# Where block 1 normalises x, and which engines split the expert biases

## The reference

```python
y = xf * lax.rsqrt(jnp.mean(xf * xf, axis=-1, keepdims=True) + RMS_EPS)
return (y * g.astype(jnp.float32)).astype(x.dtype)        # rmsnorm
gu = xblk @ w_gate_up[e] + b_gate_up[e]                    # per expert, 32 experts, 4 per token
gate = jnp.minimum(gu[:, :D_EXPERT], SWIGLU_LIMIT)
up = jnp.clip(gu[:, D_EXPERT:], -SWIGLU_LIMIT, SWIGLU_LIMIT)
act = gate * jax.nn.sigmoid(SWIGLU_ALPHA * gate) * (up + 1)
return act @ w_down[e] + b_down[e]
```

## Time and profile before

| | us |
|---|---|
| median of 3 runs (lowest, highest) | 1533.14 (1532.16, 1533.45) |
| the profiled execution | 1532.21 |
| its span | 1530.3 |
| TensorE busy (matmul), share of the span | 1444.2, 94% |
| VectorE busy | 325.5, 21% |
| ScalarE busy | 216.8, 14% |
| GpSimd busy | 21.5, 1% |
| mean granted TensorE clock | 0.981 |

### The profile page before, as it was taken

The page is one execution under the profiler, slowest core; times in us unless marked ns, Lnnn a source line. Parts: engine busy times, 40 slices in busy tenths (PEclk is TensorE's granted clock), DMA queues, the critical chain, the costliest instruction groups (busy, mean ns, idle before and its releaser), DMA issues.

```text
span 1530.3 us, 17933 instructions
## 1 busy us (share of the span) xinstructions
PE 1444.2 (94%) x7236; PEld 780.0 (51%) x7236; DVE 325.5 (21%) x864; ACT 216.8 (14%) x398; POOL 21.5 (1%) x14
## 2 busy tenths in 40 slices
PE   7999999999999999999999999999699996999998
PEld 5655444444344343334334334334498854888843
DVE  5535311111121111111112112111313344000001
ACT  1321011111111011111101101111213331100000
POOL 3200000000000000000000000000000000000000
PEclk9998999999999999999999999999799996999999
DMA  9997899999999999999999999999943221444400
GB/s 325 354 416 292 340 425 430 427 430 427 429 428 429 428 429 428 427 430 427 430 428 429 427 429 427 430 429 428 316 143 127 84 84 55 138 146 157 137 0 27
DMA packets 82569, 496.95 MB, mean 325 GB/s; under 512 B 6237, under 2 KB 47914, under 8 KB 54666
## 3 DMA queue, kind: packets, MB, share of 16 engines
q1 hardware_dynamic: 81932, 495.46, 79.7%
q10 hardware_dynamic: 606, 1.06, 0.2%
HBM read 495.44 MB, written 1.05 MB: 324 GB/s over the span
## 4 chain that ended last, share of the span: by engine, by line
PE 60%; DMA 34%; DVE 4%; ACT 1%; issue 1%; SPq 0%; DVEq 0%; ACTq 0%
DMA ring<-in_w_gate_up_dram 33%; PE PS L821 16%; PE PS L1137 10%; PE PS L930 6%; PE PS L847 5%; PE PS L1144 5%; PE PS L807 3%; PE PS L713 2%; PE PS L855 2%; PE PS L1012 2%; PE PS L665 2%; PE PS L543 1%; PE PS L560 1%; DVE pt L1566 1%; DMA ring<-in_w_ada_dram 1%
## 5 line engine op out<-in xcount | busy, mean ns | idle before, releaser
L821 PE MATMUL PS<-ring,work 128*64 128x512 f32 x2048 | 451.7, 596 | 13.7 <-DMA ring<-in_w_gate_up_dram 13.6
L821 PEld LDWEIGHTS PS<-ring,work 128*64 128x64 f32 x2048 | 145.2, 137 | 302.5 <-issue 259.9
L847 PE MATMUL PS<-ring,work 128*64 128x512 f32 x1024 | 225.1, 592 | 0.0
L1823 DVE TENSOR_SCALAR work<-PS 128x512 f32<-128x512 f32 x32 | 22.1, 692 | 660.7 <-PE PS L821 660.7
L1137 PE MATMUL PS<-cols,ring 128*128 128x256 f32 x704 | 155.4, 384 | 2.1 <-issue 2.1
L1137 PEld LDWEIGHTS PS<-cols,ring 128*128 128x128 f32 x704 | 135.8, 193 | 22.0 <-DVE cols L1527 2.5
L847 PEld LDWEIGHTS PS<-ring,work 128*64 128x64 f32 x1024 | 72.0, 137 | 131.7 <-issue 129.3
L807 PE MATMUL PS<-work,rows 128*128 128x64 f32 x1056 | 124.9, 278 | 0.0
L807 PEld LDWEIGHTS PS<-work,rows 128*128 128x128 f32 x1056 | 123.8, 196 | 0.8 <-DVE work L1801 0.8
L930 PE MATMUL PS<-ring,cols 128*128 128x240 f32 (+1 forms) x448 | 95.0, 370 | 2.1 <-DVE cols L1527 2.1
L930 PEld LDWEIGHTS PS<-ring,cols 128*128 128x128 f32 x448 | 84.9, 193 | 8.1 <-DVE cols L1527 2.5
(11 more groups left out here) (284 smaller groups left out, 919.3 us busy)
## 6 DMA issues: line engine op xcount, KB each, us to landing
ring<-in_w_gate_up_dram SPq DMA_DIRECT2D x128, 2048.0 KB, 22.1
ring<-in_w_down_dram SPq DMA_DIRECT2D x64, 2048.0 KB, 19.5
ring<-in_w_ada_dram SPq DMA_DIRECT2D x24, 1024.0 KB, 17.2
ring<-in_w_gate_up_dram SPq DMA_DIRECT2D x22, 1024.0 KB, 5.0
ring<-in_w_in_dram SPq DMA_DIRECT2D x13, 960.0 KB, 10.8
ring<-in_w_down_dram SPq DMA_DIRECT2D x11, 1024.0 KB, 4.8
ring<-in_w_out_dram SPq DMA_DIRECT2D x8, 1024.0 KB, 10.2
ring<-in_w_in_dram SPq DMA_DIRECT2D x3, 1024.0 KB, 14.4
```

Source lines behind the costliest of these rows:

```text
L821: mm = pe.matmul(bank(b)[CAP * h:CAP * (h + 1), :], xg[:, k, :], w[:, b * FE + h * 512:b * FE + (h + 1) * 512], start=False, stop=(k == KD ...
L847: mm = pe.matmul(bank(3)[CAP * h:CAP * (h + 1), :], lhs, w[:, (f % 2) * D + h * 512:(f % 2) * D + (h + 1) * 512], start=False, stop=(f == 7))
```

## The change

It has two parts.

*Block 1 turns x as it lands.* `turn_x` transposes x itself, once the constants and x0 or x1 have landed; the constants are now loaded first. VectorE takes the mean square of row tile 0 and ScalarE that of row tile 1. The column copies multiply by the gain as before. The root is computed afterwards for both tiles at once (`attn_r`), and ScalarE applies it when it copies the projected chunks out, one instruction per row tile instead of one for both. `ADA_FIRST, ADA_NEXT, ADA_MID` are 0, 2, 16: no ada chunk stands ahead of `w_in`, and eight instead of six come after the output projection.

*The expert biases.* `b_gate_up` is loaded behind the last of the 34 chunks, after the scores of the eighth head; the copies to bfloat16 are on ScalarE, ahead of the FFN norm's column copies, and the subtractions on VectorE, ahead of the residual add. GpSimd's program is gone.

Besides, three small loads signal `gfin_in` instead of a semaphore of their own, and the counts waited for are adapted (`rows_ready`, `x_squared`).

```diff
-ADA_FIRST, ADA_NEXT, ADA_MID = 2, 4, 18
+ADA_FIRST, ADA_NEXT, ADA_MID = 0, 2, 16
 # SyncE
+            load_small(cst[:, 0:CONST_FIRST], consts[:, 0:CONST_FIRST], "const_in")
             load_small(x_sb[:, 0, :], x_rows[:, 0, :], "x0_in")
             load_small(x_sb[:, 1, :], x_rows[:, 1, :], "x1_in")
-            load_small(cst[:, 0:CONST_FIRST], consts[:, 0:CONST_FIRST], "const_in")
...
-                if n == 3:
-                    for i in range(3):
-                        load_small(bgu_f[32 * i:32 * i + 32, :], ins["b_gate_up"][0], "bgu_in")
...
+            sp.wait_ge(sig["scores_done"], HEADS)
+            for i in range(3):
+                load_small(bgu_f[32 * i:32 * i + 32, :], ins["b_gate_up"][0], "bgu_in")
 # TensorE
+            def turn_x():
+                for t in range(NT):
+                    pe.wait_ge(sig[("x0_in", "x1_in")[t]], 16)
+                    for k in range(KD):
+                        mm = pe.transpose(bank(k // 2)[:, (k % 2) * T + t * P:][:, 0:P],
+                                          x_sb[:, t, k * P:(k + 1) * P], ident)
+                        if t == NT - 1 and k % 2:
+                            mm.then_inc(sig["rows_turned"], 1)
+                turned[0] += 1
...
             pe.wait_ge(sig["const_in"], 16)
+            turn_x()
...
-            for i in range(ADA_FIRST):
-                ada(i)
-            turn_rows(2)
...
             ada(ADA_MID + 3)
+            ada(ADA_MID + 4)
             pe.wait_ge(sig["x_added"], 4)
-            turn_rows(4)
-            ada(ADA_MID + 4)
+            turn_rows(2)
+            ada(ADA_MID + 5)
...
             mm.then_inc(sig["parts_done"], 1)
-            ada(ADA_MID + 5)
+            ada(ADA_MID + 6)
+            ada(ADA_MID + 7)
...
-            pe.wait_ge(sig["bias_split"], 2)
+            pe.wait_ge(sig["bias_split"], 6)
 # ScalarE
+            act.wait_ge(sig["x1_in"], 16)
+            do.tell(nc.scalar.activation(rows[:, 1, :], x_sb[:, 1, :], ACT.Square,
+                                         accum_out=stat(ms, S_ATTN)[:, 1:2]), "x_squared")
             act.wait_ge(sig["vec_cols"], 1)
+            keep_cols(lambda k: col("g_attn_norm", k))
...
-            keep_proj(proj1, IN1_CHUNKS, (4, 5), N_IN1)
+            act.wait_ge(sig["attn_r"], 1)
+            for c, (a, w) in enumerate(IN1_CHUNKS):
+                act.wait_ge(chunk_used, N_IN1 + c + 1)
+                for t in range(NT):
+                    ins_ = nc.scalar.activation(proj1[:, t, a:a + w], bank(4 + c % 2)[:, t * w:(t + 1) * w], ACT.Copy,
+                                                scale=stat(rs, S_ATTN)[:, t:t + 1])
...
-            act.wait_ge(sig["bias_split"], 1)
             for b in range(4):
...
+            act.wait_ge(sig["bgu_in"], 48)
+            act.wait_ge(sig["bdown_in"], 48)
+            for i, hi in enumerate((96, 64, 32)):
+                if i:
+                    act.wait_ge(sig["bias_left"], 2 * i - 1)
+                do.tell(nc.scalar.copy(bias_b[0:hi, :], bgu_f[0:hi, :]), "bias_split")
+                if i:
+                    act.wait_ge(sig["bias_left"], 2 * i)
+                do.tell(nc.scalar.copy(bdown_b[0:hi, :], bdown_f[0:hi, :]), "bias_split")
             keep_cols(lambda k: vcol[:, GFFN_AT + k:GFFN_AT + k + 1])
 # VectorE
-            norm_rows(S_ATTN, 0)
+            do.step(v.tensor_tensor_reduce(out=rows[:, 0, :], in0=x_sb[:, 0, :], in1=x_sb[:, 0, :], scale=1.0,
+                                           scalar=0.0, op0=ALU.mult, op1=ALU.add,
+                                           accum_out=stat(ms, S_ATTN)[:, 0:1]))
...
-            norm_rows(S_ATTN, 1)
             keep_cols(lambda k: col("g_attn_norm", k))
+            dve.wait_ge(sig["x_squared"], 1)
+            at = slice(0, NT)
+            src, dst = stat(ms, S_ATTN)[:, at], stat(rs, S_ATTN)[:, at]
+            do.step(v.tensor_scalar(src, src, 1.0 / D, EPS, ALU.mult, ALU.add))
+            rsqrt(dst, src, rsqrt_tmp[:, at])
+            do.tell(v.tensor_copy(dst, dst), "attn_r")
...
                 do.tell(v.tensor_scalar(att[:, t, :], att[:, t, :], ratio[:, t:t + 1], None, ALU.mult), "att_rows")
+            for i, hi in enumerate((64, 32)):
+                for j, (parts, full) in enumerate(((bias_b, bgu_f), (bdown_b, bdown_f))):
+                    dve.wait_ge(sig["bias_split"], 2 * i + j + 1)
+                    do.tell(v.tensor_tensor(full[0:hi, :], full[0:hi, :], parts[0:hi, :], ALU.subtract), "bias_left")
 # GpSimd: its whole block (copies and subtractions) is taken out
```

More of the change, by code:

```diff
@@ L159 @@
 out_half x_added scores_done rowmax_ready probs_ready smat_ready probs_turned pt_kept pv_done o_free att_rows att_turned att_cols
-pool_steps up_steps o_up_steps o_steps parts_done parts_kept logits_done shifted exp_ready routed ranks_done
+bias_left up_steps o_up_steps o_steps parts_done parts_kept logits_done shifted exp_ready routed ranks_done
 lists_ready bias_split
-picked sel_ready selb_ready seld_ready gathered xg_ready clipped sig_ready act_ready act_turned actt_ready yb_ready
+attn_r picked sel_ready selb_ready seld_ready gathered xg_ready clipped sig_ready act_ready act_turned actt_ready yb_ready
 sel_turned selt_ready scattered
@@ L166 @@
 moe_done x_summed x_squared z_ready r_ready x_scaled ff_ready ff_ln decay_ready cum_done cum_kept cumt_turned bias_rows conv_in conv_turned
[L167 removed]
+conv_sum conv_tanh conv_silu qk_sq heads_ready heads_turned heads_cols ml_exp ml_m ml_guard ml_tanh
 bcast_done bcast_kept y_turned y_kept gate_used silu_ready h_ready out_ready out_stored""".split()
@@ L705, in adas @@
                 return [lambda i=i: ada(i) for i in range(lo, hi)]
-            attention_1({0: adas(6, 8), 1: adas(8, 9), 2: [pool_sums] + adas(9, 10), 3: adas(10, 12), 4: adas(12, 14),
-                        5: adas(14, 16), 6: adas(16, 17), 7: adas(17, ADA_MID)})
+            attention_1({0: adas(4, 6), 1: adas(6, 7), 2: [pool_sums] + adas(7, 8), 3: adas(8, 10), 4: adas(10, 12),
+                         5: adas(12, 14), 6: adas(14, 15), 7: adas(15, ADA_MID)})
             def out_columns(base_n, c, k, t, halves=(0, 1)):
@@ L914, in _ @@
                 add_zero(4 + 2 * t, 5 + 2 * t, start=False, stop=True).then_inc(sig["moe_done"], 1)
-            turn_rows(6)
+            turn_rows(4)
             need_cols()
@@ L1084, in _ @@
             out2(1, 2)
-            pe.wait_ge(sig["rows_ready"], 7)
+            pe.wait_ge(sig["rows_ready"], 5)
             pe.wait_ge(sig["pt_kept"], heads[11][0] + 1)
@@ L1121, in _ @@
             out2(1, 7, (1,))
-            turn_rows(9)
+            turn_rows(7)
             need_cols()
@@ L1209, in _ @@
             do.tell(nc.scalar.activation(trig[:, :, :, :], trig[:, :, :, :], ACT.Sin), "trig_ready")
-            keep_proj(proj1, IN1_CHUNKS, (4, 5), N_IN1)
+            act.wait_ge(sig["attn_r"], 1)
[4 more added lines that the diff above has]
+                                                scale=stat(rs, S_ATTN)[:, t:t + 1])
+                    if t:
+                        do.tell(ins_, "proj_kept")
+                    else:
+                        do.step(ins_)
             flat_q = q_rows.rearrange("p t h n -> p t (h n)")
@@ L1708, in attention_1 @@
                           lambda t: bank(4 + t).rearrange("p (h d) -> p h d", h=HEADS))
-            attention_1({0: [lambda: keep_ada(0), square_pooled], 1: [keep_pooled], 3: [keep_pool_sums],
-                         5: [lambda: keep_ada(1)]})
+            attention_1({0: [square_pooled], 1: [keep_pooled], 2: [lambda: keep_ada(0)], 3: [keep_pool_sums],
+                         7: [lambda: keep_ada(1)]})
             st = stat(ms, S_MIX)
@@ L1890, in _ @@
                         do.step(ins_)
-            dve.wait_ge(sig["gfin_in"], 16)
+            dve.wait_ge(sig["gfin_in"], 64)
             for t in range(NT):
                 do.tell(v.tensor_tensor(z_rows[t], x_sb[:, t, :], gfin[:, :], ALU.mult), "z_ready")
-            dve.wait_ge(sig["x_squared"], 2)
+            dve.wait_ge(sig["x_squared"], 3)
             r_ = rstd(S_FINAL, D)
-            dve.wait_ge(sig["x_squared"], 4)
+            dve.wait_ge(sig["x_squared"], 5)
             st = stat(ms, S_NORM1)
@@ L1927, in _ @@
             dve.wait_ge(sig["proj_kept"], len(IN1_CHUNKS) + R_GATES)
-            dve.wait_ge(sig["bias14_in"], 48)
+            dve.wait_ge(sig["gfin_in"], 64)
             def bias_of(a, n):
@@ L2064, in _ @@
                 add_gated(0, t, "out_ready", 2, N_END)
-        @block.gpsimd
-        def _(pool):
-            steps = 0
-            for parts, full, loaded in ((bias_b, bgu_f, "bgu_in"), (bdown_b, bdown_f, "bdown_in")):
-                pool.wait_ge(sig[loaded], 48)
-                for hi in (96, 64, 32):
-                    done = sig["pool_steps"] if hi > 32 else sig["bias_split"]
-                    nc.gpsimd.tensor_copy(parts[0:hi, :], full[0:hi, :]).then_inc(done, 1)
-                    if hi > 32:
-                        steps += 1
```

(5 more changed lines are left out.)

11 lines of the change are left out of this document (4 added, 7 removed).

## The result

The changed kernel takes 1537.71 us (median of 7 runs, 1533.85 to 1542.74) against 1532.16 us of the kernel before in runs alternating with it (7 runs, 1529.23 to 1533.45): ratio 1.0041, with a 95% interval of 1.0025 to 1.0058. It is slower, by about 6 us. The forecast was 1539.0.

A forecast was written before the change was run, and what follows sets the result against it. The weight stream bounds the kernel from expert 0's first slot release. Second row tile +4.1, ada chunk +0.9 and clock +1.0 give +6.0 us on 1532.21, 1538.2; on the median 1539, own range 1535 to 1543, with rivals 1531 to 1545.

The forecast's parts named there:

- What bounds the kernel: Expert loop: the weight stream limits from 157.86 us, expert 0's first slot release; moving that moves the end equally.
- The start: Block 1 up to attention: TensorE about 6 us earlier (bounds 4 and 7.5), in-projection starting at about 11.4 us.
- The landing of the biases: Late gate/up bias load behind the last ada chunk (108.9): costs 5.2 us of stream, lands at 114.1 (110.8 to 117).
- The split: Bias copies on ScalarE and subtractions on VectorE after the landing: 9.7 us, VectorE free at 123.8 us.
- TensorE's wait for the second row tile: FFN norm: second row tile ready at 135.6 instead of 131.08, transposes done at 136.6, 4.1 us later than before.
- the clock's term: TensorE's clock from the last transposes through expert 0: +1.0 us, between 5.9 us less and 4 us more.
- Ada chunks and clock: Behind the output projection: one moved ada chunk on the path, +0.93 us; TensorE's clock, +1.0 us.
- clock returns: Rival, chance 0.13: biases late as forecast, but two ada chunks restore full clock for expert 0; +2.6 us, 1536.
- The sum: Whole kernel: second row tile +4.1, ada chunk +0.9, clock +1.0, together +6.0 us; 1538.2, forecast on the median 1539.
- Biases out of the way: Rival, chance 0.20: biases land by 105 us or VectorE's share is hidden; TensorE's path decides, 4 us faster, 1529.
- Worse of both: Rival, chance 0.11: biases land at 117 and everything up to expert 0 runs at 1.2 GHz; +12 us, 1545.
- a GpSimd that was slow but in nobody's way: Bias split before the change: GpSimd's work held nobody up; two engines replace it, one in the way.

The follow-up runs named there:

- e7: e3 with the ada chunks placed as before (six behind the output projection, not eight): 1527.56 us, ratio 0.9972.
- e1: The changed kernel with the gate/up bias loaded early and split on GpSimd, as before the change: 1532.37 us, ratio 1.0005.
- e2: The kernel before with only the bias part of the change; start and ada chunks as before: 1536.24 us, ratio 1.0048.
- e5: The changed kernel run again, nothing altered: 1538.32 us, ratio 1.0050 to the kernel before.
- e3: The changed kernel with the three gate/up bias loads issued on ScalarE's DMA queue instead of SyncE's: 1527.96 us, ratio 0.9982.
- e6: e2 with the three gate/up bias loads on ScalarE's queue: 1531.12 us, ratio 0.9997.
- e4: The changed kernel, late load on SyncE's queue kept, bias copies and subtractions on GpSimd again: 1541.79 us, ratio 1.0075.
- e9: The changed kernel, late load on SyncE kept, without VectorE's four subtractions and ScalarE's waits for them (output wrong): 1528.71 us, ratio 0.9983.

## Why the prediction was right, step by step

**What bounds the kernel.** Right. In the two profiles of the changed kernel and the ten of the variants, the time from the first release to the last expert's issue is 868.8 to 870.4 us, 869.48 before, and the span moves with the first release to within what the rest of the kernel varies: from the last of these issues to the end it is 499.9 us (e7) to 503.0 (before). So two profiles whose first releases lie less than 3 us apart can't be ranked by them. The expert at the end still takes 29.37 us.

**The start.** Forecast about 6 us earlier up to attention (4 to 7.5), worth nothing. Measured 4.9 to 5.0 in the first profile and 4.3 to 4.4 in the second: x is turned slower than priced (3.65 us for the 16 transposes instead of 1.97), and the in-projection takes 1.7 and 3.0 us longer, where I took 1 for the low clock. The step that rests on GpSimd's silence is borne out by e1, and more strongly than I priced it: 3.40 us of waiting, not 1.17. "Worth nothing" holds in e2 against e5. With the biases out of the way it seems to be worth something, by e3 against e6.

**The landing of the biases.** Forecast 114.1 (110.8 to 117). Measured 114.7 in the second profile and 118.7 in the first, outside those bounds; 113.2, 113.6 and 117.4 in e2, e4 and e9. The terms, in the second profile: the last ada chunk of this queue lands at 110.8 (89.64 + 21.2) instead of 108.9, and the last bias 3.9 us behind it instead of 5.2. Two errors of opposite sign made a good sum, which is luck. The loads do not stand behind the chunk, they share with it: the first of the three lands at 109.3, ahead of it, and the 246 GB/s of 104 to 111 us already show them. The cost to the stream is larger than I took. From 105 to 119 in the first profile 3.82 MB pass in 14 us; without the 0.79 MB of the biases, 3.03 MB at the 430 GB/s that stand there before take 7.0, so by this estimate the loads cost 7 us of stream, not 5.2. e9 says that this is free here. The Trainium skill, page "SBUF — State Buffer", section "Door 1: The DMA port swizzle", gives a load to partitions 0 to 31 half of the ports and at most about 218 GB/s. No stretch here tests this figure: the loads go to partitions 0 to 95, and of the 0.79 MB that pass from 111 to 114.5 us in the second profile, at 227 GB/s, at most 0.26 MB are biases, as two of the three have landed by 111.1. So the 198 GB/s that I said agree with it are no support either, being the rate of biases and chunks together.

**The split.** Forecast 9.7 us, ending at 123.8. Measured 10.0 from the landing (114.73 to 124.71), each piece within 0.02 us of its price, with some 0.3 us more between the pieces: 1.90 and 1.91 for the copy, 2.28 for the subtraction, 1.22 for the last. The residual add starts at 124.74.

**TensorE's wait for the second row tile.** Forecast until about 136, with the transposes done at 136.6; measured 136.63 and 138.60 in the second profile. One microsecond is VectorE's (0.9 later free), one is the half clock, at which eight transposes take 1.97 us; that was in the clock's term.

**Ada chunks and clock.** Forecast +0.93 and +1.0 (bounds -5.9 and +4). In the second profile transposes done to gather is 10.88 us (10.42 before), and gather to first release 13.83 (14.97 before). With the 1.0 us of slow transposes and less the 0.93 of the chunk the clock's term is 1.0 + 0.46 - 0.93 - 1.14 = -0.6; in the first profile, by the same steps, 1.0 + 1.53 - 0.93 - 0.53 = +1.1. Both things that I had set against each other happened: the clock comes back ahead of the routing, and is low again in the routing and in the gather. But that the two chunks in a row bring it back, as the rival *clock returns* has it, fits the first profile alone; in the second it is back before they start. So what brought it back stays open, and the rival's gain of 5.9 us did not come.

**The sum.** Second profile: 5.1 (second tile, without the clock) + 0.9 - 0.6 = 5.4, measured 5.45 at the first release. First profile: 9.1 + 0.9 + 1.1 = 11.1, measured 11.06. These sums close by construction, as the terms are stretches of one timeline; the 0.93 of the chunk is the forecast's own figure, and what it has too little or too much stands in the clock's term. What can be held against the forecast is each term: +5.1 for the second row tile where I had +4.1, and -0.6 for the clock where I had +1.0. These errors too are of opposite sign. The forecast's +6.0 is the second profile's case; the median of both sets of runs, 1537.71 and 1538.32, lies with it.

**Rivals.** *Biases out of the way* was priced 1529 with a landing before 105 as its condition: e3 made the condition true (104.1) and gives 1527.96; e9 took VectorE out of the line and gives 1528.71. *Worse of both*, priced 1545, has its time nearly met by the first profile (1542.74), but not by its terms: the landing at 118.7 is later than its 117, and the clock cost 1.1 us, not 4.

**One sentence fell.** I wrote of "a GpSimd that was slow but in nobody's way". Before, that was half true: it stretched VectorE's sums at 29 us and cost TensorE 1.17 us. In e4 it stretches VectorE on the path, and the kernel is 0.75% slower than before.

**Open.** Why the biases land at 118.7 in one execution and near 114 in the next, with the loads issued at 89.39 and 90.01, no run here settles. Nor why the clock falls for some microseconds in attention in some executions (e6) and not in others; how much of the 10 us over which the kernel before spreads comes from that was not measured.

## What to carry to other kernels

Before work is put into an idle gap of an in-order engine, ask what the engine will wait for there: a gap of 15 us on VectorE became a wait of 21.62 (17.09 in the second profile), since the operand came at the end of a deep queue, and everything behind it waited too. A small load that is wanted soon belongs on a queue with nothing ahead of it: here that took its landing from 114.7 to 104.1. An early start is worth what the last wait behind it leaves; find that wait first.

## What was not expected of the hardware

- A GpSimd operation in flight stretches VectorE's operations with two inputs in SBUF, down to one column: 128x1 from 0.16 to 3.94 us (e4), 128x1024 from 1.23 to 4.83.
- Three matmuls of 512 columns in TensorE's idle time gave back 3.3 us in the gather alone (7.09 to 3.79), and seven of 256 columns at the start 3.0 us in transposes and projection.
- The three loads of 32 partitions slow the whole stream, not only themselves: 198 GB/s before at 17 to 24 us and 412 there without them, and 245 GB/s from 96 to 104 us in e3, where they come through ScalarE's queue. Whether it is by their partitions or by their size no run here varies.
